# Where the column sums and transposes of the last first-modulation block stand on TensorE

## The reference, cut to what matters

```python
mod = c_act @ ada_w + ada_b                       # c_act = silu(c), ada_w: 2048 x 12288
sh_a, sc_a, gt_a, sh_m, sc_m, gt_m = jnp.split(mod[:, None, :], 6, axis=-1)
h = rms_norm(x, norm_mix) * (1.0 + sc_a) + sh_a   # "first modulation"
(cq, ckv, kr, fq, fk, fv, ff, nq, nkc, ...) = jnp.split(h @ w_in, split_points, axis=-1)
...                                               # three attention mixers, their norms
x = x + gt_a * (o @ w_out)
h = rms_norm(x, norm_mlp) * (1.0 + sc_m) + sh_m
x = x + gt_m * (jnp.square(jax.nn.relu(h @ mlp_w1)) @ mlp_w2)
```

## Time and profile before

| | |
|---|---|
| median of 3 runs | 2420.12 us (2419.77 to 2422.27) |
| the profiled execution | 2416.07 us |
| its span, first to last instruction | 2414.2 us |
| TensorE busy | 2311.4 us (96%) |
| DVE busy | 1704.2 us (71%) |
| ACT busy | 1136.4 us (47%) |
| mean granted TensorE clock | 0.99 of full speed |

### The profile page before, as it was taken

One profiled execution on the slowest core, in us unless ns is written; L12 is line 12 of the kernel. 1 busy time (PEld: TensorE's weight loads), 2 busy tenths in 40 slices (PEclk: granted clock), 3 DMA queues, 4 the chain that ended last, 5 costly groups with the idle time before them and its releaser, 6 DMA issues.

```text
span 2414.2 us, 29293 instructions
## 1 busy us (share of the span) xinstructions
PE 2311.4 (96%) x11145; PEld 1900.3 (79%) x11145; DVE 1704.2 (71%) x2050; ACT 1136.4 (47%) x1576; POOL 19.2 (1%) x52
## 2 busy tenths in 40 slices
PE   3798999999999999999999999999999999999998
PEld 3676678878888888888888777887888888888887
DVE  7985788879877787887767667676675555455455
ACT  3253355545544434434546445455553443443443
POOL 1000000000000000000000000000000000000000
PEclk9899999999999999999999999999999999999999
DMA  9979996889988899899878798576786666666663
GB/s 366 384 257 327 334 312 218 284 283 344 333 297 303 291 327 326 302 322 303 298 241 275 255 320 288 156 247 194 242 269 222 187 185 197 185 189 188 190 188 125
DMA packets 321075, 637.08 MB, mean 264 GB/s; under 512 B 21068, under 2 KB 43048, under 8 KB 320552
## 3 DMA queue, kind: packets, MB, share of 16 engines
q1 hardware_dynamic: 314432, 625.49, 77.1%
q10 hardware_dynamic: 6504, 9.72, 1.2%
HBM read 633.00 MB, written 2.13 MB: 263 GB/s over the span
## 4 chain that ended last, share of the span: by engine, by line
PE 84%; DVE 7%; DMA 5%; issue 2%; ACT 2%; SPq 1%; POOL 0%; ACTq 0%; DVEq 0%; POOLq 0%
PE acc L1753 18%; PE acc L1755 18%; PE acc L1754 18%; PE pair L1753 7%; PE pair L1755 7%; PE pair L1754 7%; DVE ada_acc L1214 3%; DMA w_raw<-in_w_in 2%; PE bank_T L1616 2%; DMA arena<-in_ada_w 1%; DVE w_lo L1284 1%; PE acc L1777 1%; PE pair L1804 1%; PE bank_O L1616 1%; PE pair L1812 1%
## 5 line engine op out<-in xcount | busy, mean ns | idle before, releaser
L1284 DVE TENSOR_TENSOR w_lo<-w_raw,w_hi 128x1024 fp32r<-128x1024 f32 (+3 forms) x764 | 906.3, 1190 | 408.3 <-ACT w_hi L779 407.1
L779 ACT ACTIVATE w_hi<-w_raw 128x1024 fp32r<-128x1024 f32 (+3 forms) x764 | 785.5, 1031 | 753.7 <-PE acc L1755 428.5
L1753 PE MATMUL acc<-w_hi,hT_hi 128*128 128x512 f32 (+3 forms) x1536 | 607.6, 396 | 27.0 <-DVE w_lo L1284 12.5
L1755 PE MATMUL acc<-w_lo,hT_hi 128*128 128x512 f32 (+3 forms) x1536 | 588.5, 383 | 0.0
L1754 PE MATMUL acc<-w_hi,hT_lo 128*128 128x512 f32 (+3 forms) x1536 | 587.5, 383 | 0.0
L1214 DVE SCALAR_TENSOR_TENSOR ada_acc<-w_raw,silu_c,ada_acc 128x1024 f32<-128x1024 f32 x300 | 383.6, 1279 | 1.6 <-DMA w_raw<-in_ada_w 0.8
L1753 PEld LDWEIGHTS acc<-w_hi,hT_hi 128*128 128x128 f32 x1536 | 290.9, 189 | 98.2 <-DVE w_lo L1284 24.1
L1755 PEld LDWEIGHTS acc<-w_lo,hT_hi 128*128 128x128 f32 x1536 | 290.5, 189 | 56.0
L1754 PEld LDWEIGHTS acc<-w_hi,hT_lo 128*128 128x128 f32 x1536 | 291.5, 190 | 49.7 <-issue 0.5
L1753 PE MATMUL acc<-w_hi,uT_hi 128*128 128x512 f32 (+1 forms) x656 | 256.3, 391 | 0.0
L1755 PE MATMUL acc<-w_lo,uT_hi 128*128 128x512 f32 (+1 forms) x656 | 254.6, 388 | 0.0
(11 more groups left out here) (249 smaller groups left out, 1885.3 us busy)
## 6 DMA issues: line engine op xcount, KB each, us to landing
w_raw<-in_mlp_w SPq DMA_DIRECT2D x512, 512.0 KB, 4.8
w_raw<-in_ada_w SPq DMA_DIRECT2D x320, 512.0 KB, 5.7
w_raw<-in_w_in SPq DMA_DIRECT2D x112, 512.0 KB, 5.3
arena<-in_ada_w SPq DMA_DIRECT2D x64, 512.0 KB, 11.0
w_raw<-in_w_out SPq DMA_DIRECT2D x64, 512.0 KB, 5.4
w_raw<-in_nsa_cmp_k_w SPq DMA_DIRECT2D x32, 512.0 KB, 6.7
w_raw<-in_nsa_cmp_v_w SPq DMA_DIRECT2D x32, 512.0 KB, 6.7
w_raw<-in_w_in SPq DMA_DIRECT2D x16, 388.0 KB, 5.7
```

The lines of the kernel that those rows point to most:

```text
L779: a.activation(w_hi[:, at % RING, :, 0:n], w_raw[:, i % RAW, :, 0:n], ACT.Copy).then_inc(hi_done, 1)
L1284: v.tensor_tensor(w_lo[:, at % RING, :, 0:n], w_raw[:, RING_NO["lo", Q] % RAW, :, 0:n], w_hi[:, at % RING, :, 0:n].bitcast(F32), ALU.subtr ...
L1753: pe.matmul(o, st_hi[:, kt + k, tok], wh, start=first and k == 0, stop=False)
L1755: mm = pe.matmul(o, st_hi[:, kt + k, tok], wl, start=False, stop=last and k == 1)
```

## The change

For block 3 alone (`b == 3`, so q = 18) the steps `n1_6` and `adaA3` move on TensorE from behind piece 17 to behind piece 14, and `n1_7` moves to behind piece 15. On ACT and DVE the steps that go with them move from behind piece 19 to behind piece 18. Blocks 1 and 2 stay where they were. No instruction is added or removed.

```diff
-            t_step(0, q - 1, f"n1_{2 * b}", q + 1, 1, 2.2)
-            t_step(0, q - 1, f"adaA{b}", q + 1, 0, 2)
-            t_step(0, q - 1, f"n1_{2 * b + 1}", q + 1, 0, 2.4)
+            early, at_side = (4, q) if b == 3 else (1, q + 1)
+            t_step(0, q - early, f"n1_{2 * b}", at_side, 1, 2.2)
+            t_step(0, q - early, f"adaA{b}", at_side, 0, 2)
+            t_step(0, q - max(early - 1, 1), f"n1_{2 * b + 1}", at_side, 0, 2.4)
```

## The result

| | before | with the change |
|---|---|---|
| median | 2417.96 us (20 runs, 2414.1 to 2423.6) | 2422.23 us (20 runs, 2419.2 to 2425.5) |
| ratio to before | | 1.0018, 95% interval 1.0011 to 1.0024 |
| span of the profiled execution | 2414.2 us | 2420.7 us |

The change makes the kernel slower, by 4.3 us as the medians have it and by 2.7 to 5.8 us as the interval has it (0.0011 and 0.0024 of 2418).

A forecast was written before the change was run, and what follows sets the result against it. TensorE was taken to bound the kernel, busy 2311 of 2414 us. Terms 3.54 + 3.2 + 1.12 + 4.2 + 5.5 gave 17.6 us against 12.2, so +5.4 and a median of 2425.5 us, range 2420.0 to 2428.5.

The forecast's parts named there:

- The gate: Block 3's last `ada_w` tile on DVE holds up the column sums; the change doesn't bring it forward, TensorE idles about 13 us.
- The sums: Block 3's column sums on TensorE, behind the last tile: 3.54 us after about 13 us of idle time.
- Piece 15: Its 12 matmuls, now behind the column sums on TensorE, priced at the low clock: 3.2 us.
- The second transposes: TensorE transposes behind piece 15, needing `bank_T` emptied by DVE: 1.12 us.
- Pieces 16 and 17: Behind the second transposes on TensorE, back to back at full speed: 4.2 us; 7.5 at the low clock.
- The sum: TensorE from the start of the column sums to the end of piece 19: 17.6 us against 12.2, 5.4 us later.
- ACT and DVE at nothing: The moved ACT and DVE steps cost nothing, covered by pieces 15 to 17; uncovered they would add 2 to 3 us.
- The whole delay reaches the end: From the evacuation of `cq` onward all later work shifts, so the full 5.4 us reaches the end.
- The price of the clock: Behind the last tile on TensorE: +5.4 us with a low-clock restart, +1.9 us at full speed all through.
- The first: Rival: behind the tile TensorE's clock stays or comes back early, delay 1.9 to 4.5 us, within 0.2%; chance 0.27.
- The third: Rival: TensorE's low clock lasts through piece 17, +7 to +9 us, 2427 to 2429 us; chance 0.08.
- The second: Rival: loads between 200 and 300 us take the delay up, kernel not slower, 2420 down to 2417 us; chance 0.14.

The follow-up runs named there:

- two kernels with a smaller dose: The change with block 3's sums moved only behind piece 15, or only behind piece 16, against the kernel before: ratios 1.0011 and 1.0009.
- ACT and DVE half alone: Kernel before with only the ACT and DVE steps moved ahead of the splits of piece 19, TensorE order unchanged: ratio 1.0000, median -0.4 us.
- TensorE half alone: Kernel before with only the TensorE steps moved, ACT and DVE order unchanged: ratio 1.0033, median +7.5 us.
- experiment with the clock kept up: The changed kernel plus 95 useless 256-column products in TensorE's idle time ahead of block 3's sums, against the kernel before: ratio 1.0003, median +1.6 us.
- delay of 18 us: Kernel before plus 150 useless 256-column products on TensorE between block 3's last tile and its sums: ratio 1.0083, median +18.5 us.

## Why the prediction was right, point by point

- **The gate.** It said that the tile is not brought forward and TensorE idles from 110.5 to 123.5. It idled from 110.5 to 122.94, with the wait put down to L1215.
- **The sums.** 3.54 us forecast by block 0, 3.55 measured; piece 15 starts 3.4 us behind their start. A wait of 6.41 us gave the same 3.54, one of 0.94 filled with work gave 1.95.
- **Piece 15.** 3.2 forecast, 3.4 measured from 126.35 to 129.70.
- **The second transposes.** 1.12 forecast, 0.70 measured (129.70 to 130.40). The row's 1.05 is a modelled duration, of which 0.35 lies beside the next piece. This term was too large by 0.4.
- **Pieces 16 and 17.** 4.2 forecast, 5.2 measured (130.40 to 135.55). This is the term that was mis-sized most in this execution. The step was "so I price them low and the rest high": the low clock was to hold for the 4.3 us of piece 15 and the transposes. It held until past 132.15 us, which is 5.8 us of dense work. In the two kernels with a smaller dose, whose sums were as slow, it held for 3.0 us. So how long it holds was luck of the execution or something that these runs don't show. (The 7.5 us that the prediction gave both pieces at the low level are a little short: the first two steps of piece 16 in its rows are still faster than the later 0.32 us, and 24 x 0.32 is 7.7.)
- **Pieces 18 and 19.** 5.5 forecast and 5.5 measured (135.55 to 141.03).
- **The sum.** 18.1 us against 17.6 forecast and 12.2 before. L945 was forecast at about 141.3 and started at 141.31; that close a hit is luck, since the tile was 0.5 us earlier than in the profile before, and with the tile where it had been L945 would have started at about 141.8.
- **ACT and DVE at nothing.** Right for the change and for its ACT and DVE half alone (1.0000). "If that cover were gone, they would add 2 to 3 us" was tested once, with the sums behind piece 16, and there it was less: a wait of 1.37 us. The 3.0 us of the TensorE half alone are another thing. There the steps on ACT and DVE stood in their old place, behind the splits of piece 19, and held up the second transposes.
- **The whole delay reaches the end.** Right. Local time and median moved together: +0.5 and -0.4, +1.5 and +1.6, +2.4 and +2.3, +2.9 and +2.6, +5.9 and +4.3, +8.9 and +7.5, +19.8 and +18.5 us. The median is up to 1.6 us lower for the larger ones. The local times lie inside the intervals of the ratios but for that of the change, 5.9 against an upper end of 5.8. One reading fits it: with 3.0 us of dense work at the low level in place of 5.8, as in the two smaller doses, the local time would be 1.4 us shorter, 4.5, close to the median's 4.3. That is an estimate from one profile of each kernel. Whether the profiled execution was slow in this stretch, or a microsecond is given back later, the runs don't settle.
- **The price of the clock.** The prediction gave 5.4 with the low clock and 1.9 with full speed behind the tile, both against the kernel before as it was. The experiment with the clock kept up gave a local +1.5 and a median of +1.6. The Trainium skill's rule ("TensorE: Matmul & The Clock Gate", section "HAM oscillation — how this bites in real kernels"), that an idle wait between bursts makes the next burst start at the low clock, is borne out here: 12.40 us of idle time, then 0.50 of the granted clock for nine microseconds of work.
- **The rivals.** The first, that the clock stays or comes back early, named the sums as its sign, below 2.4 us. They took 3.55, so its mechanism is out. But its price, a delay of 1.9 to 4.5 us within 0.2%, holds the measured 4.3 us, while the forecast's own 4.8 to 6.5 us holds only the local 5.9. The third, that the low clock lasts through piece 17, was half right: it lasted into piece 16. The second, that the loads take the delay up, is ruled out at its size by the delay of 18 us.
- **The signs of being wrong.** None came: the sums started at 122.94, not later than 123.6, piece 18 at 135.55, not before 133, and the distance from L945 to the end grew by 1.1 us (2278.3 to 2279.4).

The change measured 4.3 us where 5.4 were forecast, and it is slower by 0.18%, a little under the 0.2% that I had named as the least that a measurement can tell. So by size the result lies just within the 0.2% that the prediction gave 0.41, and not in the "slower by over 0.2%" that it gave 0.53, although the mechanism is that of the forecast. With 20 runs on each side the measurement tells it apart all the same: the interval, from 1.0011 to 1.0024, doesn't hold 1.

## What to carry to other kernels

Work that needs nothing from the thing that is late belongs ahead of the wait, not behind it: the three pieces were free where they stood, and behind the tile they cost their lost cover. Moving them also emptied the engine for 12 us, and the slow restart cost nearly as much as the lost cover did (2.7 against 3.2 us of the local time, by one profile of each kernel; the medians don't settle the split). The kernel before had some low clock of its own, so what a restart costs is seen only when both kernels are run with the clock kept up. Read what an engine does *during* a wait that you lengthen, and price the restart with a row of the same trace.

## What the runs showed of the hardware that I had not expected

- Once low, TensorE's clock stayed at 1.2 GHz through 3.5 us of column sums and then 5.8 us of dense products. How long it lasts does not follow the length of the idle time ahead in these profiles: the dense products left the low level after 3.0 us behind waits of 6.41 and 10.59 us, after 5.8 behind 12.40, and, with waits of 1.5 to 2.0 us right ahead, after 2.7 (before), 4.9 (the ACT and DVE half alone) and 5.3 us (the kernel with the delay).
- 18.87 us of continuous products did not protect what came 2 us later. In the kernel with the delay piece 18 started at 147.16, after 1.98 us of idle time, with the sums and the second transposes before it, and the clock was low again:

```profile
147.00:152.00 5.00, 4.84 (x11) 3.80 (x12) 3.77 (x15) 2.17 (x4) 0.00 (x0) 0.50 0.27 75
```

- Short products don't get cheaper with their width. 256 columns took 0.122 us each (11.63 / 95), 128 columns 0.117 (4.46 / 38). Each has its own weight load, 0.19 us on average in both traces, so the load and not the width seems to set the pace; that was not tried apart.
